# Delta rule with two heads' chunk halves exchanged, out0's split in two parts, and the last squares taken per chunk

## The reference

```python
    sol = lax.linalg.triangular_solve(amat, rhs, left_side=True, lower=True, unit_diagonal=True)
    u, w = sol[..., :DV], sol[..., DV:]
    attn = jnp.einsum('nbhik,nbhjk->nbhij', q, k) * decay

    def step(S, xs):
        qc, kc, uc, wc, gcc, ac = xs
        v_new = uc - jnp.einsum('bhck,bhkv->bhcv', wc, S)
        o = (jnp.einsum('bhck,bhkv->bhcv', qc * jnp.exp(gcc)[..., None], S)
             + jnp.einsum('bhij,bhjv->bhiv', ac, v_new))
        g_last = gcc[..., -1]
        S = (S * jnp.exp(g_last)[..., None, None]
             + jnp.einsum('bhck,bhcv->bhkv', kc * jnp.exp(g_last[..., None] - gcc)[..., None], v_new))
        return S, o
```

## Time and profile before

| | us |
|---|---|
| median of 3 runs (lowest, highest) | 1595.12 (1592.93, 1599.3) |
| the profiled execution | 1595.45 |
| its span | 1593.7 |
| mean granted clock of TensorE | 0.994 |

### The profile page before, as it was taken

One profiled execution on the slowest core, in us unless ns is written; L12 is line 12 of the kernel. 1 busy time (PEld: TensorE's weight loads), 2 busy tenths in 40 slices (PEclk: granted clock), 3 DMA queues, 4 the chain that ended last, 5 costly groups with the idle time before them and its releaser, 6 DMA issues.

```text
span 1593.7 us, 31820 instructions
## 1 busy us (share of the span) xinstructions
PE 1561.0 (98%) x13520; PEld 1506.6 (95%) x13520; DVE 644.7 (40%) x1210; ACT 568.2 (36%) x999; POOL 633.3 (40%) x533
## 2 busy tenths in 40 slices
PE   8999999999999999999999999999999999999998
PEld 8999988878998999999999998699899999999998
DVE  4485146355425422223223534834264223232244
ACT  5133255344336422313223313844354223132232
POOL 3755203323552443544534542035424444443441
PEclk9999999899999999999999999999999999999999
DMA  5222211003340232232223224013412223223221
GB/s 149 91 87 81 82 56 61 2 2 124 101 159 28 80 103 84 80 100 87 80 84 102 80 87 141 2 54 106 133 43 91 80 81 106 80 80 107 80 80 57
DMA packets 123061, 131.85 MB, mean 83 GB/s; under 512 B 6285, under 2 KB 115122, under 8 KB 122930
## 3 DMA queue, kind: packets, MB, share of 16 engines
q1 hardware_dynamic: 118128, 125.24, 24.5%
q10 hardware_dynamic: 4802, 4.66, 0.9%
HBM read 122.44 MB, written 7.45 MB: 82 GB/s over the span
## 4 chain that ended last, share of the span: by engine, by line
PE 48%; issue 31%; POOL 17%; DVE 2%; ACT 1%; DMA 1%; POOLq 0%; ACTq 0%; DVEq 0%
PE LP L839 38%; POOL wl L729 17%; PE LP L1229 3%; PE MP L995 1%; PE LP L944 1%; DMA stage<-in_w_in_ab 1%; PE MP L968 1%; PE LP L1171 0%; PE MP L1321 0%; PE MP L1069 0%; PE MP L1229 0%; PE MP L1213 0%; PE MP L1330 0%; PE MP L1205 0%; PE MP L1086 0%
## 5 line engine op out<-in xcount | busy, mean ns | idle before, releaser
L729 POOL TENSOR_TENSOR wl<-stage,wh 128x512 fp32r<-128x512 f32 x428 | 578.4, 1384 | 796.4 <-ACT wh L1611 784.0
L839 PE MATMUL LP<-xh,wh 128*128 128x272 f32 x2112 | 440.6, 290 | 3.9 <-DVE xl L2172 2.9
L839 PE MATMUL LP<-xh,wl 128*128 128x272 f32 x2112 | 437.2, 288 | 0.0
L839 PE MATMUL LP<-xl,wh 128*128 128x272 f32 x2112 | 435.7, 288 | 0.0
L1611 ACT CAST wh<-stage 128x2048 fp32r<-128x2048 f32 x107 | 204.0, 1906 | 441.1 <-PE LP L839 412.9
L839 PEld LDWEIGHTS LP<-xh,wh 128*128 128x128 f32 x2112 | 332.3, 188 | 6.2 <-DVE xl L2172 3.9
L839 PEld LDWEIGHTS LP<-xl,wh 128*128 128x128 f32 x2112 | 332.1, 189 | 0.0
L839 PEld LDWEIGHTS LP<-xh,wl 128*128 128x128 f32 x2112 | 330.0, 189 | 0.0
L839 PE MATMUL LP<-hh,wh 128*128 128x272 f32 x1024 | 211.3, 287 | 0.0
L839 PE MATMUL LP<-hh,wl 128*128 128x272 f32 x1024 | 210.5, 288 | 0.0
L839 PE MATMUL LP<-hl,wh 128*128 128x272 f32 x1024 | 210.3, 287 | 0.0
(11 more groups left out here) (419 smaller groups left out, 1678.0 us busy)
## 6 DMA issues: line engine op xcount, KB each, us to landing
stage<-in_w_up SPq DMA_DIRECT2D x32, 1024.0 KB, 5.4
stage<-in_w_down SPq DMA_DIRECT2D x32, 1024.0 KB, 5.2
stage<-in_w_in_ab SPq DMA_DIRECT2D x13, 1024.0 KB, 5.4
stage<-in_w_xkv SPq DMA_DIRECT2D x8, 1024.0 KB, 5.1
stage<-in_w_in_c SPq DMA_DIRECT2D x6, 1024.0 KB, 5.0
stage<-in_w_out_ab SPq DMA_DIRECT2D x4, 1024.0 KB, 10.6
stage<-in_w_xq SPq DMA_DIRECT2D x4, 1024.0 KB, 5.4
stage<-in_w_xo SPq DMA_DIRECT2D x4, 1024.0 KB, 5.2
```

Source lines behind the costliest of these rows:

```text
L729: pool.tensor_tensor(wl[s][:, part], stage[s][:, part], wh[s][:, part].bitcast(f32), ALU.subtract).then_inc(w_lo, 1)
L839: mm = pe.matmul(LP[:, 2 * slot + half, 0:b - a], weights, X[part][k][:, a:b], start=(first and n_ == 0), stop=(last and n_ == 2), skip_gr ...
```

## The change

Heads 2 and 3 exchange the halves of a tile: their first chunk lies on partitions 64 to 127 and their second on 0 to 63. So in each chunk step heads 0, 1 work on one half and heads 2, 3 on the other, and SPREAD = [0, 2, 1, 3] issues them alternately.

- The exchange is made where ScalarE writes the conv's result (two Silu operations by half for 6 of the 12 rows), in the gates (flips: four operations in place of one, twice) and in the decay of the state (three exponentials in place of one). Turning back is done in VectorE's multiplication with z: three operations in place of one.
- ws is four matmuls of 64 output rows for w (w_bank, half of bank 1), a signal, a wait for rec_act, and four for q (o_bank, half of bank 3). Both chunks of a tile now use this one o_bank. The wait of ws for an earlier copy is gone.
- vnew, o_rows, um: two heads side by side on 128 partitions instead of four on 64.
- ds puts heads 0, 1 in bank 1 and heads 2, 3 in bank 2.
- The upper half of out0's first panel (rows of FoX) is split before x16 of round one, and its low part made behind GpSimd's masks of round one. The lower half stays where the whole was. TensorE's pieces wait for fox_lo, the heads' rows for w_lo.
- Of the last tile's four squares, two stand behind o of (3,0) instead of o of (3,1), and their unread result goes to um[0].

```diff
-            behind["o", j, 1] += [norm("sq", j, h) for h in range(H)] + [norm("rs", j), norm("mul", j), ("turn", "o", j),
-                                                                        norm("hi", j), norm("lo", j)]
+            behind["o", j, 0] += [norm("sq", j, 0), norm("sq", j, 1)]
+            behind["o", j, 1] += [norm("sq", j, 2), norm("sq", j, 3), norm("rs", j), norm("mul", j), ("turn", "o", j),
+                                  norm("hi", j), norm("lo", j)]
...
+        sample_bank, w_bank, o_bank = MP[:, 3, :], MP[:, 1, 0:256], MP[:, 3, 0:256]
+
+        def update_bank(h):
+
+            at = 256 + 128 * (h % FLIPPED)
+            return MP[:, 1 + h // FLIPPED, at:at + 128]
...
+        FLIPPED = H // 2
+        SPREAD = [h + FLIPPED * i for h in range(FLIPPED) for i in range(2)]
...
+        def home(h, c):
+
+            return c if h < FLIPPED else 1 - c
...
             for what in DELTA:
+                if what == ("inv", "uw", 0):
+                    for j in (0, 1, TT):
+                        pool.wait_ge(inv_pool[STREAM[j]], len(sizes_of(j)))
+                    pool.wait_ge(fox_hi, 1)
+                    for i in range(PIECES // 2, PIECES):
+                        part = slice(i * 2048 // PIECES, (i + 1) * 2048 // PIECES)
+                        pool.tensor_tensor(wl[0][:, part], stage[0][:, part], wh[0][:, part].bitcast(f32),
+                                           ALU.subtract).then_inc(fox_lo, 1)
+                    pool.wait_ge(fox_lo, PIECES // 2)
...
-                        pe.wait_ge(rec_act, max(q - 1, 1))
...
+                    if j < TT:
+                        for h in SPREAD:
+                            half, to = home(h, c), 128 * (h % FLIPPED)
+                            mm = pe.matmul(w_bank[chunks_of(j)[half], to:to + 128],
+                                           wq[j][:, h, 192 * half:192 * half + 64], S[:, old, h, :],
+                                           start=(h % FLIPPED == 0), stop=True, skip_group_check=True)
+                        mm.then_inc(rec_pe, 1)
+                        pe.wait_ge(rec_act, q)
+                        for h in SPREAD:
+                            half, to = home(h, c), 128 * (h % FLIPPED)
+                            pe.matmul(o_bank[chunks_of(j)[half], to:to + 128],
+                                      wq[j][:, h, 64 + 64 * half:128 + 64 * half], S[:, old, h, :],
+                                      start=(h % FLIPPED == 0), stop=False, skip_group_check=True)
+                        return
...
-                    for h in range(H):
-                        mm = pe.matmul(MP[:, 2, 128 * h:128 * h + 128], kd[j][p, h, :], vnew[p, h, :],
+                    for h in SPREAD:
+                        p, n_ = home_rows(j, h, c), h % FLIPPED if j < TT else h
+                        mm = pe.matmul(update_bank(h), kd[j][p, h, :], vnew[p, n_, :],
                                        start=True, stop=True, skip_group_check=True)
...
-                pe.wait_ge(w_lo, PIECES * LIN["out0"][0] + k * PIECES // KT + 1)
+                pe.wait_ge(fox_lo, k * PIECES // KT + 1 - PIECES // 2)
...
             for what in DELTA:
+                if what == ("inv", "x16", 0):
+                    act.wait_ge(w_loaded[0], 16 * (LIN["out0"][0] // 2 + 1))
+                    act.copy(wh[0][:, 1024:2048], stage[0][:, 1024:2048]).then_inc(fox_hi, 1)
                 if what == ("rec", "ws", 2, 0):
                     act.wait_ge(rec_pe, 1)
-                    split(0, 16 * (LIN["out0"][0] // 2 + 1))
+                    act.copy(wh[0][:, 0:1024], stage[0][:, 0:1024]).then_inc(w_hi, 1)
...
-                    dve.tensor_tensor(vnew[p, :, :], um[j][p, :, :],
-                                      state_bank(c)[p, :].rearrange("p (h n) -> p h n", h=H),
-                                      ALU.subtract).then_inc(rec_dve, 1)
+                    if j < TT:
+                        dve.tensor_tensor(vnew[:, 0:2, :], um[j][:, 2 * c:2 * c + 2, :],
+                                          w_bank.rearrange("p (s n) -> p s n", s=2),
+                                          ALU.subtract).then_inc(rec_dve, 1)
```

More of the change, by code:

```diff
@@ L212, in build_program @@
         gate_tmp = more("gate_tmp", [128, NTOK, GATES])
-        gates = more("gates", [128, NTOK, GATES])
+        gates_all = more("gates_all", [128, NTOK, GATES])
+        gates = gate_tmp
         lf_past = more("lf_past", [128, PAST // 128, H])
@@ L560, in chunks_of, with flips, home_rows, out_slot @@
             return [slice(c * WIDTH[j], (c + 1) * WIDTH[j]) for c in range(2 if j < TT else 1)]
+        FLIPPED = H // 2
+        SPREAD = [h + FLIPPED * i for h in range(FLIPPED) for i in range(2)]
+        def flips(at):
+            straight, turned_ = slice(at, at + FLIPPED), slice(at + FLIPPED, at + H)
+            return [(gates[:, 0:TT, straight], gates_all[:, 0:TT, straight]),
+                    (gates[0:64, 0:TT, turned_], gates_all[64:128, 0:TT, turned_]),
+                    (gates[64:128, 0:TT, turned_], gates_all[0:64, 0:TT, turned_]),
+                    (gates[:, TT, at:at + H], gates_all[:, TT, at:at + H])]
+        def home(h, c):
+            return c if h < FLIPPED else 1 - c
+        def home_rows(j, h, c):
+            return chunks_of(j)[home(h, c) if j < TT else c]
+        def out_slot(j, h, c):
+            return 2 * c + h % FLIPPED if j < TT else h
         def crossed(j):
@@ L820, in _ @@
                     level_mask(what[2], SIZES.index(int(what[1][1:])) + 1)
-            low_parts(0, LIN["out0"][0] + 1)
+            pool.wait_ge(w_hi, LIN["out0"][0] + 1)
+            for i in range(PIECES // 2):
+                part = slice(i * 2048 // PIECES, (i + 1) * 2048 // PIECES)
+                pool.tensor_tensor(wl[0][:, part], stage[0][:, part], wh[0][:, part].bitcast(f32), ALU.subtract
+                                   ).then_inc(w_lo, 2)
             pool.wait_ge(rec_pe, 3 * len(CHUNKS))
@@ L1292, in inverse @@
                     pe.wait_ge(turn_used, max(TURNS.index(("k", j)), TURNS.index(("v", j))) + 1)
-                    for h, p in each():
-                        mm_(b0[p, 128 * h:128 * h + 128], TmT[s][p, h, :], vbt[j][p, h, :])
+                    for h, c in [(h, c) for h in range(H) for c in range(len(parts))]:
+                        p, to = home_rows(j, h, c), 128 * out_slot(j, h, c)
+                        mm_(b0[p, to:to + 128], TmT[s][p, h, :], vbt[j][p, h, :])
                     for h in range(H):
@@ L1349, in head_parts @@
                 pe.wait_ge(low_done, NTOK - 1 + half)
+                pe.wait_ge(w_lo, PIECES * (LIN["out0"][0] + 1))
                 a, b = TOKENS[half]
@@ L1748, in conv_row @@
                 act.wait_ge(conv_dve, CW * (f + 1))
-                act.activation(ua[:, f, 0:NPT], conv_sum[:, f % 2, 0:NPT], ACT.Silu)
+                if f % H < FLIPPED:
+                    act.activation(ua[:, f, 0:NPT], conv_sum[:, f % 2, 0:NPT], ACT.Silu)
+                else:
+                    by_half = [v.rearrange("p (j c n) -> p j c n", j=TT, c=2)
+                               for v in (ua[:, f, 0:NPT], conv_sum[:, f % 2, 0:NPT])]
+                    for c in range(2):
+                        act.activation(by_half[0][:, :, 1 - c, :], by_half[1][:, :, c, :], ACT.Silu)
                 act.activation(ua[:, f, NPT:N], conv_sum[:, f % 2, NPT + PAD:NPT + PAD + NS], ACT.Silu
@@ L1863, in _ @@
                 act.activation(gsm[0:P, part, 4:12].rearrange("p j (t h) -> p t j h", t=2), sums(P, 0, 2), ACT.Exp)
-                nch = 2 if P == 128 else 1
-                inst = act.activation(eg[:, part, 0:nch, :].rearrange("p j c h -> p c j h"), sums(128, 2, nch), ACT.Exp)
+                if P < 128:
+                    inst = act.activation(eg[:, part, 0, :], sums(128, 2, 1)[:, 0, :, :], ACT.Exp)
+                else:
+                    act.activation(eg[:, part, :, 0:FLIPPED].rearrange("p j c h -> p c j h"),
+                                   sums(128, 2, 2)[:, :, :, 0:FLIPPED], ACT.Exp)
+                    for c in range(2):
+                        act.activation(eg[:, part, c, FLIPPED:H], sums(128, 3 - c, 1)[:, 0, :, FLIPPED:H], ACT.Exp)
             inst.then_inc(sum_act, 1)
@@ L1951, in _ @@
                     split(1, 16 * (LIN["out0"][0] // 2 + 1))
-                if what == ("norm", "sq", TT - 1, 0):
+                if what == ("norm", "sq", TT - 1, FLIPPED):
                     act.nop().then_inc(arena_free, 1)
@@ L2418, in turn_in @@
                     dve.wait_ge(turn_done, use + 1)
-                    dve.scalar_tensor_tensor(out=z[:, :, a:a + P],
-                                             in0=MP[:, 0, 0:H * P].rearrange("p (h n) -> p h n", h=H),
-                                             scalar=column(ONORM), in1=z[:, :, a:a + P], op0=ALU.mult, op1=ALU.mult
-                                             ).then_inc(turn_used, 1)
+                    if j < TT:
```

(9 more changed lines are left out.)

61 lines of the change are left out of this document (39 added, 22 removed).

## The result

The changed kernel takes 1583.49 us (median of 6 runs, 1582.7 to 1584.94) against 1595.54 for the kernel before beside it. One of its six runs, of 1699.86 us, was slow and is not in the ratio; the median of the other five is 1595.12. The ratio is 0.993, 95% interval 0.9919 to 0.994: 11 to 12 us, 0.7% faster. The time lies inside the range, 0.9 us above its lower end, on the side of rival B.

The account below looks back on a forecast made before the run. TensorE, busy 98% of the span, was taken to bound the kernel, with gains only where it waits, runs at half clock or gets less work. 3.3 + 3.1 - 0.2 = 6.2 us off gave 1589.2 us; range 1582.6 to 1596.

Parts of the forecast that it names:

- rival B: Round two: one half-clock piece, just after the stall at 326.76, goes; 3.3 us more gained, 1585.9 us; chance 0.27.
- Half-width products: Delta rule's products: alternating array halves lets records overlap, so a group of 8 shrinks by 0.45 us.
- the last four chunks: Chunks (2,0) to (3,1), to the last state update: done at 16.7 us instead of 19.83, gain 3.1 us.
- Rival C: State products: column halves do not overlap, costing 6.3 us over seven chunks, 1595.5 us; chance 0.07.
- The ring: One chunk's cycle from state products to next state products: falls from 4.30 us by 1.16 to 3.14.
- The walk: Step-by-step timing of the last four chunks from 352.83 as zero: (2,1)'s update products 5.1, (3,0)'s w 7.9, end 16.7.
- the wait for the output bank: Chunk (3,0): o's half of the state products waits 0.75 us for ScalarE's copy of the previous chunk's output.
- Round two: Second round of the inverse with interleaved state updates: 3.5 from TensorE's load, 0.3 from z's wait, 0.5 back; gain 3.3 us.
- The tail: Stretch behind the last state update: nothing gained beyond the recurrence's 3.1 us, as loads move only with it; bounds 0 and 0.4.
- ScalarE's cast in round one: Half cast of out0's panel ahead of three copies of the inverse: costs 0.2 us, bounds 0 and 0.95.
- The clock: TensorE's granted clock: no gain in the sum; round two's was to stay within 0.05 of 0.85.
- the sum: Whole kernel: round two 3.3 plus last four chunks 3.1 less ScalarE's cast 0.2, together 6.2 us gained.

Follow-up runs that it names:

- serial order: Changed kernel with heads issued 0, 1, 2, 3: in all groups 1585.56 us, ratio 0.9947; in the state products alone 1584.53 us, ratio 0.994.
- the early split alone: Kernel before plus only the earlier split of the upper half of out0's first panel: 1593.51 us, ratio 0.9995.
- the changed kernel again: Changed kernel measured and profiled once more without any edit, on the same chip as the other experiments: 1583.56 us, ratio 0.9923.
- the fillers: Unused identity products, five in each of two TensorE waits: kernel before 1590.16 us (first wait alone 1591.41, second alone 1592.39), changed kernel 1581.39 us.

## Why the prediction was right in its parts and short in its sum

**Half-width products: right in size, wrong in reason.** 8 records were to last 0.7 us and last 0.61 to 0.71. In the grouped view, 32 records of the last four chunks took 4.6, 4.4 and 4.3 us busy before, and now 2.9 (update), 2.6 and 2.5 (two state groups for one) and 2.6 (output). Grouped rows of before:

```profile
L1326 PE MATMUL MP<-vnew,kd 64*128 64x128 f32 x32 | 4.6, 285 | 0.8 <-DVE vnew L2473 0.8
L1321 PE MATMUL MP<-S,wq 128*128 128x128 f32 x32 | 4.4, 281 | 0.2 <-DVE S L2479 0.2
```
and of after:

```profile
L1379 PE MATMUL MP<-vnew,kd 64*128 64x128 f32 x32 | 2.9, 297 | 0.1
L1361 PE MATMUL MP<-S,wq 128*64 128x128 f32 x32 | 2.6, 285 | 0.6 <-DVE S L2574 0.6
```
The mean of one record has hardly changed (285 and 281 ns, now 297 and 285); they overlap more. Rival C is excluded. Wrong was the reason given, that neighbours must alternate: in serial order the groups of this form last 0.66 to 0.72 us.

**The ring and the last four chunks: right.** 3.14 predicted, 3.12 measured. The walk gave update products at 5.1, (3,0)'s state products at 7.9 and the end at 16.7 us; they came at 5.10, 7.86 and 16.43. The missing 0.3 is the wait for the output bank: 0.75 predicted, 0.36 measured, since z ended at 7.89 rather than 8.0 and the copy started at 8.45 (353.96), not at 8.65, and took 0.37.

**Round two: right without the clock.** Lost clock taken off, it takes 47.7 and 44.5 us: 3.2 gained, 3.3 predicted. It repeats: 47.9 us with the early split alone, 44.3 in the changed kernel again. But 5.2 us of clock come on top in these two profiles, about 4 in the mean of the runs over the whole span. Rival B named this (one piece gone: 3.3) and gave it 0.27. Its reason did not hold: the wait of 1.11 us that was to be shortened stands as it was (1.12 us), and the kernel with the early split alone has that wait too and no half clock behind it. B's size was near, by luck as far as the runs show.

**The tail: the term that was wrong.** "Nothing beyond the 3.1 passes; bounds 0 and 0.4"; measured 1.1. Before, TensorE waited 1.07, 0.72 and 0.77 us there, and now 0.79 and 0.99: 0.8 less. The last output products lasted 1.08 us and now 0.65: 0.4. Both are on TensorE's path, and m_rows ceased to be waited for: GpSimd's low part of the next panel starts right behind those output products and frees the buffer for the load behind it. Its start came 373.19 - 372.66 = 0.53 us after the last state before and 0.10 after. I had halved the output products "on TensorE" and then not carried that into the tail. In the other four profiles of kernels with the old delta rule this stretch takes 24.1 to 24.4 us, and 23.3 to 23.4 in all nine of the new, so the change is worth 0.7 to 1.1 there. That the squares had no share is shown; the rest of the chain is read from the traces and wasn't tested alone.

**ScalarE's cast in round one: 0.2 charged, nothing seen.** Before round two the changed kernel gained 0.7 us in the first pair of profiles, clock taken off. It can't be put down to the change: clock taken off, this stretch takes 294.2 to 296.7 us in the profiles of the new layout and 294.1 to 294.9 in those of the old, so neither the 0.2 nor the 0.7 can be told there.

**The clock.** Over the whole span the profiles lose 10.2 us before and 6.9 after: 3.4 of the 12.7, much as in the mean of the runs (10.8 and 6.8). The other 9.3 are the stretches': 3.2, 3.4, 1.1, then 0.7 ahead of round two and 0.9 in the rest, for which I have no cause. Other kernels with the old delta rule have 1195.3 to 1195.8 us in the rest, so the 0.9 is hardly the change's.

The step that failed is therefore the sum's silence on clock and tail: it put the clock at nothing, where the runs show about 4 us, and the tail at nothing, where 0.7 to 1.1 came. I held the loss of a piece for a rival because one trace could not show which stall brought it. The traces of the fillers show that the wait of 1.04 us brings half clock; but the changed kernel still has that wait, so why it loses less clock than before stays open. Without the clock the runs gained 7.5 us (0.9 either way) where the sum had 6.2.

## What to carry to other kernels

When products use half of the rows or columns of the array, put them on both halves: a group's time nearly halves (1.16 to 0.66 us here), with four heads in serial order almost as with alternating ones, and a recurrence gains it several times over. In a ring, follow each shortened group to the end of the stretch, also the one behind the last step. A wait of 1 us on TensorE can cost several more in clock, though not every such wait does: look at the granted clock right behind it in more than one profile, average the clock over the runs, and try idle products in it before rearranging anything.

## What was not expected of the hardware

- Adding ten unused products made the kernel before 4.8 us faster (0.9971, 0.9961 to 0.9981).
- The same kernel shows its half-clock pieces at different places and lengths from one execution to the next: the changed kernel lost 1.7 us at 154 us and 1.7 near 312 in one profile, nothing at 154 and 3.4 near 312 in the other:

```profile
152.00:160.00 8.00, 8.00 (x73) 7.95 (x73) 1.86 (x6) 2.27 (x4) 5.01 (x4) 1.00 0.03 5
```
- Weights of 128 rows and 64 columns into the two column halves overlap as those of two row halves do: 8 loads of the state products took 0.42 us. Before, 8 of 128 columns took 0.97, and 8 of the same 64 columns, all on one half, 0.84:

```profile
345.51 0.42 PEld L1361 LDWEIGHTS MP<-S,wq 128*64 128x64 f32 x8
```
```profile
352.83 0.97 PEld L1321 LDWEIGHTS MP<-S,wq 128*128 128x128 f32 x8
...
355.85 0.84 PEld L1330 LDWEIGHTS MP<-vnew,AT 64*64 64x64 f32 x8
```
